# The score products of a channel tile's two heads, issued as six matmuls in turn on rows 0-63 and 64-127

## The chip, the cores and the metric

The kernel runs on one core of one Trainium2 chip. The metric is the device time of one launch in microseconds (us), median of the runs. Engines: PE is TensorE (its weight loads are listed apart as PEld), DVE VectorE, ACT ScalarE, POOL GpSimd, SP the engine that issues most DMAs. Each engine works through its own instructions in order; they wait for one another by semaphores.

## The reference: what is computed

One layer of a decoder for a prompt of 512 tokens and 8 sample tokens, width 2048. One input projection gives queries, keys and values (16 heads of 64 channels), indexer queries (16 heads of 64), one indexer key of 64 and a weight per indexer head, pooling inputs and gates. An indexer scores every visible key,

```
s = einsum('bthi,bsi->bths', qi, ki) * IDX_DIM ** -0.5
I = einsum('bths,bth->bts', relu(s), wi)
```

and each prompt token keeps the 128 best keys of its causal range. Attention over these (scores q.k / 8, softmax, times v), a pooling mixer, two gates, an output projection and a feed-forward network of width 8192 with squared ReLU follow. For the prompt the kernel computes all scores of a block of 128 queries against the keys up to that block's end (128, 256, 384 or 512 of them) and adds a bias of -1e30 where a key was not kept.

## The kernel before

All products are made of three matmuls: each operand is split into a high and a low part, and high x high, low x high and high x low are summed in one PSUM bank. Projections come in units of 128 output channels: 16 k-slots (`unit`, L1811), in each of which three products go into two halves of 260 tokens, six matmuls of 260 columns in all; for indexer queries (`index_unit`, L1835) three matmuls of 392 columns in one piece, since the first 128 tokens keep all their keys and need no scores. Channels lie on the 128 partitions, so a channel tile of a query or key holds two heads: head 0 on rows 0-63, head 1 on rows 64-127.

Other work of PE is put between the k-slots by hand, as hooks: PE's instructions have the order in which they are written.

**Indexer stage** (some 175 to 290 us). For channel tile j (8 of them) and query block i = 1, 2, 3 with 256, 384 and 512 keys, `index_steps` issues one step for each head: `split_product`, three matmuls of 64 rows (L1821), in the order `ISTEPS` (all i of head 0, then all i of head 1), at k-slots 4, 6, 8, 10, 12, 14 of the next tile's unit. Step c = 6j + n writes bank c % 4. ACT takes it with a Relu into buffer c % 4 (L798, `s_irl`), DVE multiplies by the head's weight and adds to the block's bias (L1387, `s_iac`). PE waits until the Relu of step c - 4 is done, ACT until the addition of step c - 4 is done, DVE until its own addition three steps before is done. ACT makes the high part of the next weights (L731) and POOL the low part (L1100) in the same stage.

**Attention rounds** (some 440 to 870 us). Four rounds, each with two channel tiles. Eight units run in a round (two each of q, k, v and a gate), and 16 score steps x = 0 to 15 (`STEPS`: tile jj, block i = 0 to 3, head hh innermost) hang between their k-slots. The list `TIMELINE` holds due times in k-slots: score step x is due at 77.3 + 2.8 x, its exponential 1.5 later, its transposes ("turn", L2004) 4.9 later, the product with the values ("pv", L2011) 8.2 or 9.1 later, and after both heads of a block the transpose of the output ("oT", L2017) 10.0 after the odd step. PE, ACT and DVE each issue their parts in the order of this list. Score step x writes bank x % 2; DVE adds the bias and takes the maximum (L1471, signalled by `s_mx`, which stands one ahead), ACT makes the exponential in place (L863), PE transposes it, DVE copies it (L1479). Before score step x PE waits for `s_mx` = max(x, 1), which means that the maximum of step x - 2 is done and its bank is free.

Of the kernel before, what the change touches and what calls it, by code (L numbers as in the profile page):

```python
# [32 lines left out]
P = 128  # L33
# [7 lines left out]
HD = 64  # L41
# [50 lines left out]
def program(nc, x_prompt, x_sample, cache_k, cache_v, cache_kidx, state_pool, page_table, norm_mix_g, w_in,  # L92
# [5 lines left out]
    def sem(name):  # L98
        return ctx.enter_context(nc.semaphore(name))
# [8 lines left out]
    def at(name, shape, dt, off):  # L108
        return nc.alloc_sbuf_tensor_at(name, shape, dt, offset=base + off)
# [42 lines left out]
    qih = at("qih", [P, NJ, SEQ], F32R, R2)  # L152
    qil = at("qil", [P, NJ, SEQ], F32R, R2 + 16640)
# [22 lines left out]
    kih = at("kih", [P, SEQ], F32R, SM + 1312)  # L176
    kil = at("kil", [P, SEQ], F32R, SM + 1312 + 2048)
    qh = at("qh", [P, 2, SEQ], F32R, R2C + 5120)
    ql = at("ql", [P, 2, SEQ], F32R, R2 + 16640)
    kh = at("kh", [P, 2, SEQ], F32R, R2 + 20736)  # L180
    kl = at("kl", [P, 2, SEQ], F32R, R2 + 24832)
# [91 lines left out]
    AB = ctx.enter_context(nc.psum_tensor("AB", [P, 4, 512], F32))  # L273
# [67 lines left out]
    s_isc = sem("indexer_products")  # L341
    s_irl = sem("indexer_relu")
    s_iac = sem("indexer_accumulated")
# [10 lines left out]
    s_sc = sem("scores_ready")  # L354
    s_mx = sem("scores_maximum_ready")
# [144 lines left out]
    def qi_sample(rows, slot):  # L500

        few = HC - HP
        return PP[rows, slot, 0, HP - P:QI_N].rearrange("p (a b) -> p a b", b=few)[:, 0:HC // few + 1:HC // few, :]

    ISTEPS = [(i, hh) for hh in range(2) for i in range(1, 4)]

    STEPS = [(jj, i, hh) for jj in range(2) for i in range(4) for hh in range(2)]

# [210 lines left out]
    def _(act):  # L719
# [71 lines left out]
        def index_relus(j):  # L791
            for n, (i, hh) in enumerate(ISTEPS):
                c = 6 * j + n
                act.wait_ge(s_isc, c + 1)
                if c >= 4:
                    act.wait_ge(s_iac, c - 3)
                w = P * (i + 1)
                act.activation(rl[c % 4][:, 0:w], AB[:, c % 4, 0:w], ACT.Relu).then_inc(s_irl, 1)  # L798
# [461 lines left out]
    def _(dve):  # L1260
# [82 lines left out]
        for j in range(NJ):  # L1343
            u, g = 2 * N_U + j, j // 2
            w = 2 << g
# [22 lines left out]
        for j in range(NJ):  # L1368
            u = 2 * N_QI + j
            dve.wait_ge(s_ps[j // 2], 16)  # L1370
            dve.wait_ge(s_qih, j + 1)
            for to, cols in QI_PROMPT:
                dve.tensor_tensor(qil[:, j, to], PP[:, u % 2, 0, cols], qih[:, j, to].bitcast(F32), ALU.subtract)
            dve.tensor_copy(qiB[0:HD, 0, 0, j, :].rearrange("p (f c) -> p f c", f=2), qi_sample(slice(0, HD), u % 2))
            dve.tensor_copy(qiB[HD:P, 1, 1, j, :].rearrange("p (f c) -> p f c", f=2), qi_sample(slice(HD, P), u % 2))\
                .then_inc(drained[u % 2], 1)
            if j == 0:
                group_out(3)
            for n, (i, hh) in enumerate(ISTEPS):
                c, w = 6 * j + n, P * (i + 1)  # L1380
                col = wN[:, i, hh * 8 + j:hh * 8 + j + 1]
                dve.wait_ge(s_irl, c + 1)
                if j + hh == 0:
                    ins = dve.tensor_scalar(blk_bias[i], rl[c % 4][:, 0:w], col, None, ALU.mult)
                else:
                    dve.wait_ge(s_iac, c - 2)
                    ins = dve.scalar_tensor_tensor(out=blk_bias[i], in0=rl[c % 4][:, 0:w], scalar=col,  # L1387
                                                   in1=blk_bias[i], op0=ALU.mult, op1=ALU.add)
                ins.then_inc(s_iac, 1)
# [45 lines left out]
        with dve.Fori(0, QKV_IT) as it:  # L1435
            order.enter(it, 16)
            for t, kind, x in TIMELINE:
                if kind == "drain" and x[0] < 6:
                    u, jj = 2 * N_QKV + x[0], x[0] % 2
# [26 lines left out]
                elif kind == "score":  # L1466
                    jj, i, hh = STEPS[x]
                    w = P * (i + 1)
# [5 lines left out]
                elif kind == "turn":  # L1474
                    jj, i, hh = STEPS[x]
                    w = P * (i + 1)
# [3 lines left out]
                elif kind == "pv":  # L1480
                    jj, i, hh = STEPS[x]
# [4 lines left out]
                elif kind == "oT":  # L1486
                    jj, i, hh = STEPS[x]
# [31 lines left out]
        for g in range(2 * NB):  # L1519
            b, f = g // 2, g % 2  # L1520
# [268 lines left out]
    def _(pe):  # L1789
# [25 lines left out]
                    if hooks and e == 0 and k in hooks:  # L1815
                        hooks[k]()

        def split_product(out, sta, stas, mov, movs):

            for n, (a, b) in enumerate(((0, 0), (1, 0), (0, 1))):  # L1820
                mm = pe.matmul(out, sta(stas[a]), mov(movs[b]), start=(n == 0), stop=(n == 2))  # L1821
            return mm

        def z(k):
            return zh[:, k], zl[:, k]
# [16 lines left out]
        def before(u):  # L1842
            return [(u + 1) // 2, u // 2]
# [59 lines left out]
            unit(2 * N_U + j, "wide", z, before(2 * N_U + j), hooks=hooks)  # L1903

        def index_steps(j):
            def step(n):
                i, hh = ISTEPS[n]
                c, r = 6 * j + n, HD * hh
                if n == 0:
                    pe.wait_ge(drained[j % 2], (2 * N_QI + j) // 2 + 1)  # L1910
                if c == 0:
                    pe.wait_ge(s_grpd, 4)
                    pe.wait_ge(s_kid, 32)
                if c >= 4:
                    pe.wait_ge(s_irl, c - 3)
                split_product(AB[:, c % 4, 0:P * (i + 1)], lambda t: t[r:r + HD, j, P * i:P * i + P], (qih, qil),
                              lambda t: t[r:r + HD, 0:P * (i + 1)], (kih, kil)).then_inc(s_isc, 1)

            return {4 + 2 * n: (lambda n=n: step(n)) for n in range(6)}

        for j in range(NJ):
            hooks = index_steps(j - 1) if j else {}
# [45 lines left out]
        for m in range(2, 6):  # L1968
            b = 2 * m - 4
# [6 lines left out]
        for it in range(0, QKV_IT):  # L1976
            def a3_turn(kind, x):
                pe.wait_ge(s_a3d, it * A3_PER + (A3_AT[(kind, x)] + 1))

            def side(kind, x):  # L1980
                if kind == "knat":
                    a3_turn(kind, x)
                    pe.wait_ge(drained[x % 2], it * 4 + ((2 * N_QKV + 2 + x) // 2 + 1))
                    for t in range(4):
                        mm = pe.transpose(AB[:, 3, P * t:P * t + P], kT[:, x, P * t:P * t + P], ident[:, :])
                    mm.then_inc(s_a3, 1)
                elif kind == "vnat":
                    a3_turn(kind, x)
                    pe.wait_ge(drained[x % 2], it * 4 + ((2 * N_QKV + 4 + x) // 2 + 1))
                    for t in range(4):  # L1990
                        mm = pe.transpose(AB[:, 3, P * t:P * t + P], vT[:, P * t:P * t + P], ident[:, :])
                    mm.then_inc(s_a3, 1)
                elif kind == "score":
                    jj, i, hh = STEPS[x]
                    pe.wait_ge(s_mx, it * 16 + max(x, 1))
                    r = HD * hh
                    split_product(AB[:, x % 2, 0:P * (i + 1)], lambda t: t[r:r + HD, jj, P * i:P * i + P], (qh, ql),
                                  lambda t: t[r:r + HD, jj, 0:P * (i + 1)], (kh, kl)).then_inc(s_sc, 1)
                elif kind == "turn":
                    jj, i, hh = STEPS[x]  # L2000
                    pe.wait_ge(s_ex, it * 16 + (x + 1))
                    pe.wait_ge(s_ptd, it * 16 + (x + 1))
                    for t in range(i + 1):
                        mm = pe.transpose(AB[:, 2, P * t:P * t + P], pr[:, x % 2, P * t:P * t + P], ident[:, :])  # L2004
                    mm.then_inc(s_pt, 1)
                elif kind == "pv":
                    jj, i, hh = STEPS[x]
                    a3_turn(kind, x)
                    pe.wait_ge(s_ptd, it * 16 + (x + 2))
                    for t in range(i + 1):  # L2010
                        mm = pe.matmul(AB[:, 3, 0:HD], pT[:, x % 2, P * t:P * t + P],  # L2011
                                       vn[:, jj, t, HD * hh:HD * hh + HD], start=(t == 0), stop=(t == i))
                    mm.then_inc(s_a3, 1)
                elif kind == "oT":
                    jj, i, hh = STEPS[x]
                    a3_turn(kind, x)
                    pe.transpose(AB[:, 3, 0:P], on[:, i, :], ident[:, :]).then_inc(s_a3, 1)  # L2017

            events = [(k, x) for _, k, x in TIMELINE if k not in ("drain", "top", "exp")]

            groups, unit_of = {}, None
            for k, x in events:
                if k == "unit":
                    unit_of = x
                    groups[x] = []
                else:
                    groups[unit_of].append((k, x))
            for n in range(8):
                hooks = {s: (lambda g=groups[(n, s)]: [side(k, x) for k, x in g]) for s in range(16) if groups[(n, s)]}
                unit(2 * N_QKV + n, "wide", z, before(2 * N_QKV + n), it, 8, 4, hooks)  # L2030
# [191 lines left out]
        for t in range(5):  # L2222
# [4 lines left out]
            for m in range(0 if t else KD - 2, KD):  # L2227
                mm = y_turn(t, m)
# [30 lines left out]
```

## Time and profile before

| | |
|---|---|
| median of 3 runs (lowest, highest) | 2936.05 us (2935.62, 2936.62) |
| the profiled execution | 2935.32 us |
| its span, first to last instruction | 2933.6 us |
| PE busy | 2856.2 us (97%) |
| DVE busy | 1425.0 us (49%) |
| ACT, POOL busy | 863.7, 858.1 us (29% each) |
| mean granted clock of PE | 0.994 |

The busy time of PE is the time in which at least one matmul is in flight, not the time in which it does all it can. The row of a matmul gives its start as the profile records it, and an end that is modelled; the starts of neighbours tell more than the durations. "x2" in a row of the timeline stands for two like instructions behind one another, and the start is that of the first. `64*128 64x256` is a matmul with a stationary operand of 64 rows and 128 columns, and a moving operand of 64 rows and 256 columns. In brackets stands idle time of the engine ahead of an instruction, and what ended it.

### The profile page before, as it was taken

The page shows a single profiled execution, that of the slowest core. Times are in us where ns is not written, and L with a number is a line of the kernel's source. Part 1 is how long each engine was busy: PE and PEld are TensorE (multiplying, and loading weights), DVE is VectorE, ACT ScalarE, POOL GpSimd, SP SyncE. Part 2 cuts the span into 40 slices and gives each one's busy share as a digit, 9 for nine tenths or more (in the row PEclk, how much of TensorE's full clock was granted, in tenths as well). Part 3 has the DMA queues.
Part 4 walks back from the last instruction along what each step waited for, and adds up shares of the span by engine and source line. Part 5 has one row for each costly group of instructions (what it writes and reads, how often), then busy time and mean ns, then how long its engine had stood idle before and what let it go on. Part 6 is the DMA issues. An engine that isn't in the chain of part 4 may idle for free.

```text
span 2933.6 us, 53028 instructions
## 1 busy us (share of the span) xinstructions
PE 2856.2 (97%) x22735; PEld 2774.2 (95%) x22735; DVE 1425.0 (49%) x2194; ACT 863.7 (29%) x1063; POOL 858.1 (29%) x280
## 2 busy tenths in 40 slices
PE   6999999999999999999989999999999999999997
PEld 6988999999999989999979999999989999999997
DVE  4555863646545404332167777777763223222212
ACT  4133222222222114223343444444432222222212
POOL 2333432332326533433300000000024444444431
PEclk9999999999999999999999999999999999999999
DMA  5222332323227644434424344344363233332321
GB/s 187 98 83 91 99 98 76 98 69 101 69 76 258 201 144 141 130 127 130 127 80 137 117 144 133 120 145 127 126 225 137 87 116 116 116 134 97 116 101 59
DMA packets 268734, 354.75 MB, mean 121 GB/s; under 512 B 9706, under 2 KB 199346, under 8 KB 267225
## 3 DMA queue, kind: packets, MB, share of 16 engines
q1 hardware_dynamic: 232067, 296.01, 30.5%
q10 hardware_dynamic: 29262, 30.28, 3.1%
q0 software_dynamic: 7200, 25.30, 2.5%
q8 instruction: 180, 2.95, 0.4%
q14 instruction: 25, 0.20, 0.0%
HBM read 310.55 MB, written 41.19 MB: 120 GB/s over the span
## 4 chain that ended last, share of the span: by engine, by line
PE 84%; issue 6%; DVE 4%; POOL 2%; ACT 1%; DMA 1%; DVEq 1%; ACTq 0%; POOLq 0%; SPq 0%
PE PP L1811 53%; PE PP L2178 18%; PE AB L2178 3%; PE PP L1835 3%; PE AB L1821 3%; POOL lo L1100 2%; PE AB L2011 1%; PE AB L2069 1%; DVE prod L1523 1%; PE AB L2004 1%; DMA qb<-q_scratch 1%; PE AB L1896 0%; DVE craw L1730 0%; ACT AB L752 0%; DVE scS L1458 0%
## 5 line engine op out<-in xcount | busy, mean ns | idle before, releaser
L1100 POOL TENSOR_TENSOR lo<-raw,hi 128x2048 fp32r<-128x2048 f32 x168 | 798.8, 4755 | 1938.3 <-ACT hi L731 1257.7
L731 ACT ACTIVATE hi<-raw 128x2048 fp32r<-128x2048 f32 x168 | 321.3, 1913 | 627.0 <-PE PP L1811 608.5
L1811 PE MATMUL PP<-zh,hi 128*128 128x260 f32 x2080 | 442.5, 294 | 2.0 <-DVE dheld L1312 1.1
L1811 PE MATMUL PP<-fh,hi 128*128 128x260 f32 x2048 | 413.6, 283 | 7.2 <-issue 5.0
L1811 PE MATMUL PP<-zh,lo 128*128 128x260 f32 x2080 | 419.4, 283 | 0.0
L1811 PE MATMUL PP<-zl,hi 128*128 128x260 f32 x2080 | 419.2, 283 | 0.0
L1811 PE MATMUL PP<-fh,lo 128*128 128x260 f32 x2048 | 413.4, 284 | 0.0
L1811 PE MATMUL PP<-fl,hi 128*128 128x260 f32 x2048 | 412.7, 283 | 0.0
L1622 DVE TENSOR_TENSOR lo<-raw,hi 128x1024 fp32r<-128x1024 f32 x224 | 274.4, 1226 | 158.8 <-ACT hi L991 158.8
L1811 PEld LDWEIGHTS PP<-zh,hi 128*128 128x128 f32 x2080 | 320.6, 189 | 19.4 <-issue 14.7
L1763 DVE TENSOR_TENSOR h<-PP,h 128x520 f32<-128x520 f32 x128 | 89.5, 700 | 500.6 <-PE PP L1811 500.6
L1811 PEld LDWEIGHTS PP<-fh,hi 128*128 128x128 f32 x2048 | 316.2, 189 | 8.1 <-issue 6.4
L1811 PEld LDWEIGHTS PP<-zh,lo 128*128 128x128 f32 x2080 | 321.4, 189 | 0.0
L1811 PEld LDWEIGHTS PP<-zl,hi 128*128 128x128 f32 x2080 | 321.1, 189 | 0.0
L991 ACT ACTIVATE hi<-raw 128x1024 fp32r<-128x1024 f32 x224 | 237.2, 1061 | 279.0 <-DVE raw L1639 75.7
L1811 PEld LDWEIGHTS PP<-fh,lo 128*128 128x128 f32 x2048 | 316.5, 189 | 0.0
L1811 PEld LDWEIGHTS PP<-fl,hi 128*128 128x128 f32 x2048 | 315.5, 189 | 0.0
L742 ACT COPY held<-eps 1x1 f32<-1x1 f32 x113 | 21.3, 189 | 363.9 <-PE PP L1811 253.5
L1811 PE MATMUL PP<-mgh,hi 128*128 128x260 f32 x512 | 104.7, 286 | 0.1
L1811 PE MATMUL PP<-mgh,lo 128*128 128x260 f32 x512 | 103.1, 283 | 0.0
L1811 PE MATMUL PP<-mgl,hi 128*128 128x260 f32 x512 | 103.1, 283 | 0.0
L2178 PE MATMUL PP<-a,hi 128*128 128x260 f32 x512 | 95.3, 286 | 5.8 <-DVE stg L1692 5.8
(387 smaller groups left out, 5406.0 us busy)
## 6 DMA issues: line engine op xcount, KB each, us to landing
raw<-in_w_in_dram SPq DMA_DIRECT2D x36, 2048.0 KB, 9.0
raw<-in_w_up_dram SPq DMA_DIRECT2D x32, 2048.0 KB, 9.0
raw<-in_w_down_dram SPq DMA_DIRECT2D x32, 2048.0 KB, 8.0
ffn_scratch<-stg SPq DMA_DIRECT2D x32, 520.0 KB, 2.8
craw<-ffn_scratch SPq DMA_DIRECT2D x16, 1040.0 KB, 6.5
raw<-in_w_out_dram SPq DMA_DIRECT2D x8, 2048.0 KB, 9.7
gates_scratch<-gst ACTq DMA_DIRECT2D x32, 260.0 KB, 3.5
raw<-in_w_attn_out_dram SPq DMA_DIRECT2D x8, 1024.0 KB, 5.4
```

What stands on the lines that cost most here:

```text
L731: act.activation(part(hi, kind, u), raw_unit(kind, u), ACT.Copy).then_inc(hi_done, 1)
L991: act.activation(ring_hi[i % 4], up_weights(s, pos), ACT.Copy).then_inc(up_hi, 1)
L1100: pool.tensor_tensor(part(lo, kind, u), raw_unit(kind, u), part(hi, kind, u).bitcast(F32), ALU.subtract)\
L1523: dve.tensor_tensor(prod[:, :], kv[:, g % 4, :], qb[:, b % 2, :], ALU.mult).then_inc(s_kvu, 1)
L1622: dve.tensor_tensor(ring_lo[i % 4], up_weights(s, pos), ring_hi[i % 4].bitcast(F32), ALU.subtract)\
L1763: dve.tensor_tensor(hm, PP[:, e, :, 0:HC], hm, ALU.add).then_inc(drained[e], 1)
L1811: mm = pe.matmul(PP[:, slot, f, 0:HC], w[:, k, P * e:P * e + P], a[:, f, :], start=(k == 0 and n == 0), stop=(k == nk - 1 and n == 2))
L1821: mm = pe.matmul(out, sta(stas[a]), mov(movs[b]), start=(n == 0), stop=(n == 2))
L1835: mm = pe.matmul(PP[:, u % 2, 0, 0:QI_N], w[:, k, :], a, start=(k == 0 and n == 0), stop=(k == KD - 1 and n == 2))
L2004: mm = pe.transpose(AB[:, 2, P * t:P * t + P], pr[:, x % 2, P * t:P * t + P], ident[:, :])
L2011: mm = pe.matmul(AB[:, 3, 0:HD], pT[:, x % 2, P * t:P * t + P], vn[:, jj, t, HD * hh:HD * hh + HD], start=(t == 0), stop=(t == i))
L2178: mm = pe.matmul(out, w[:, k, :], a, start=(k == 0 and n == 0 and not onto), stop=(k == KH - 1 and n == 2), skip_group_check=onto or opens)
```

## The change

`split_product` goes, and `head_pair` comes in its place. It issues the three products of both heads in turn: high x high of head 0 on rows 0-63, the same of head 1 on rows 64-127, then low x high of both, then high x low of both. The two heads write two banks, and the last matmul of each head signals by itself.

In the indexer stage `ISTEPS` has the head innermost, so that the steps c and c + 1 are the two heads of one block. There are three pairs for a tile, at k-slots 4, 8 and 12. A pair waits until the Relus up to step c - 3 are done. DVE waits, for head 1, until its addition for head 0 (the instruction before) is done, and for head 0 until the one of the same block in the tile before.

In the attention rounds a pair is issued at the due time of its even step; at the odd one PE issues nothing. The pair waits until the maximum of step x - 1 is done, so that both banks are free. The orders of DVE and ACT stay.

```diff
--- before.py
+++ after.py
@@ -502,7 +502,7 @@
         few = HC - HP
         return PP[rows, slot, 0, HP - P:QI_N].rearrange("p (a b) -> p a b", b=few)[:, 0:HC // few + 1:HC // few, :]
 
-    ISTEPS = [(i, hh) for hh in range(2) for i in range(1, 4)]
+    ISTEPS = [(i, hh) for i in range(1, 4) for hh in range(2)]
 
     STEPS = [(jj, i, hh) for jj in range(2) for i in range(4) for hh in range(2)]
 
@@ -1383,7 +1383,7 @@
                 if j + hh == 0:
                     ins = dve.tensor_scalar(blk_bias[i], rl[c % 4][:, 0:w], col, None, ALU.mult)
                 else:
-                    dve.wait_ge(s_iac, c - 2)
+                    dve.wait_ge(s_iac, c if hh else c - 4)
                     ins = dve.scalar_tensor_tensor(out=blk_bias[i], in0=rl[c % 4][:, 0:w], scalar=col,
                                                    in1=blk_bias[i], op0=ALU.mult, op1=ALU.add)
                 ins.then_inc(s_iac, 1)
@@ -1815,11 +1815,14 @@
                     if hooks and e == 0 and k in hooks:
                         hooks[k]()
 
-        def split_product(out, sta, stas, mov, movs):
+        def head_pair(outs, sta, stas, mov, movs, done):
 
             for n, (a, b) in enumerate(((0, 0), (1, 0), (0, 1))):
-                mm = pe.matmul(out, sta(stas[a]), mov(movs[b]), start=(n == 0), stop=(n == 2))
-            return mm
+                for hh, out in enumerate(outs):
+                    rows = slice(HD * hh, HD * hh + HD)
+                    mm = pe.matmul(out, sta(stas[a], rows), mov(movs[b], rows), start=(n == 0), stop=(n == 2))
+                    if n == 2:
+                        mm.then_inc(done, 1)
 
         def z(k):
             return zh[:, k], zl[:, k]
@@ -1903,20 +1906,20 @@
             unit(2 * N_U + j, "wide", z, before(2 * N_U + j), hooks=hooks)
 
         def index_steps(j):
-            def step(n):
-                i, hh = ISTEPS[n]
-                c, r = 6 * j + n, HD * hh
-                if n == 0:
+            def step(m):
+                i, c = m + 1, 6 * j + 2 * m
+                w = P * (i + 1)
+                if m == 0:
                     pe.wait_ge(drained[j % 2], (2 * N_QI + j) // 2 + 1)
                 if c == 0:
                     pe.wait_ge(s_grpd, 4)
                     pe.wait_ge(s_kid, 32)
                 if c >= 4:
-                    pe.wait_ge(s_irl, c - 3)
-                split_product(AB[:, c % 4, 0:P * (i + 1)], lambda t: t[r:r + HD, j, P * i:P * i + P], (qih, qil),
-                              lambda t: t[r:r + HD, 0:P * (i + 1)], (kih, kil)).then_inc(s_isc, 1)
-
-            return {4 + 2 * n: (lambda n=n: step(n)) for n in range(6)}
+                    pe.wait_ge(s_irl, c - 2)
+                head_pair([AB[:, (c + hh) % 4, 0:w] for hh in range(2)], lambda t, r: t[r, j, P * i:P * i + P],
+                          (qih, qil), lambda t, r: t[r, 0:w], (kih, kil), s_isc)
+
+            return {4 + 4 * m: (lambda m=m: step(m)) for m in range(3)}
 
         for j in range(NJ):
             hooks = index_steps(j - 1) if j else {}
@@ -1992,10 +1995,11 @@
                     mm.then_inc(s_a3, 1)
                 elif kind == "score":
                     jj, i, hh = STEPS[x]
-                    pe.wait_ge(s_mx, it * 16 + max(x, 1))
-                    r = HD * hh
-                    split_product(AB[:, x % 2, 0:P * (i + 1)], lambda t: t[r:r + HD, jj, P * i:P * i + P], (qh, ql),
-                                  lambda t: t[r:r + HD, jj, 0:P * (i + 1)], (kh, kl)).then_inc(s_sc, 1)
+                    if hh == 0:
+                        w = P * (i + 1)
+                        pe.wait_ge(s_mx, it * 16 + (x + 1))
+                        head_pair([AB[:, x, 0:w] for x in range(2)], lambda t, r: t[r, jj, P * i:P * i + P],
+                                  (qh, ql), lambda t, r: t[r, jj, 0:w], (kh, kl), s_sc)
                 elif kind == "turn":
                     jj, i, hh = STEPS[x]
                     pe.wait_ge(s_ex, it * 16 + (x + 1))
```

## Rows read from the trace of the kernel before

**Rows 1.** Busy time by stretch: length, PE, PEld, DVE, ACT, POOL, clock, DMA.

```profile
175.00:290.00 115.00, 114.91 (x581) 90.73 (x582) 55.79 (x76) 41.70 (x72) 33.77 (x12) 1.00 0.25 80
440.00:870.00 430.00, 426.54 (x3332) 403.32 (x3330) 229.71 (x621) 106.66 (x184) 123.99 (x27) 1.00 0.26 83
```

**Rows 2.** The page's chain of waits, shares of the span by line.

```profile
PE PP L1811 53%; PE PP L2178 18%; PE AB L2178 3%; PE PP L1835 3%; PE AB L1821 3%; POOL lo L1100 2%; PE AB L2011 1%; PE AB L2069 1%; DVE prod L1523 1%; PE AB L2004 1%; DMA qb<-q_scratch 1%; PE AB L1896 0%; DVE craw L1730 0%; ACT AB L752 0%; DVE scS L1458 0%
```

**Rows 3.** Timeline of PE, first score step; columns: start, duration, engine, line, operation.

```profile
442.07 0.41 PE L1811 MATMUL PP<-zh,lo 128*128 128x260 f32 x2
442.40 0.32 PE L1821 MATMUL AB<-kh,qh 64*128 64x128 f32 x1
442.57 0.27 PE L1821 MATMUL AB<-kh,ql 64*128 64x128 f32 x1
442.68 0.27 PE L1821 MATMUL AB<-kl,qh 64*128 64x128 f32 x1
442.88 0.51 PE L1811 MATMUL PP<-zh,hi 128*128 128x260 f32 x2
443.23 0.40 PE L1811 MATMUL PP<-zl,hi 128*128 128x260 f32 x2
```

**Rows 4.** Timeline of PE, indexer steps of 256 and 512 keys.

```profile
188.85 0.34 PE L1835 MATMUL PP<-zh,lo 128*128 128x392 f32 x1
189.12 0.38 PE L1821 MATMUL AB<-kih,qih 64*128 64x256 f32 x1
189.35 0.28 PE L1821 MATMUL AB<-kih,qil 64*128 64x256 f32 x1
189.47 0.27 PE L1821 MATMUL AB<-kil,qih 64*128 64x256 f32 x1
...
189.96 0.34 PE L1835 MATMUL PP<-zl,hi 128*128 128x392 f32 x1
...
192.66 0.34 PE L1835 MATMUL PP<-zh,lo 128*128 128x392 f32 x1
192.93 0.49 PE L1821 MATMUL AB<-kih,qih 64*128 64x512 f32 x1
193.26 0.39 PE L1821 MATMUL AB<-kih,qil 64*128 64x512 f32 x1
193.49 0.39 PE L1821 MATMUL AB<-kil,qih 64*128 64x512 f32 x1
...
194.10 0.34 PE L1835 MATMUL PP<-zl,hi 128*128 128x392 f32 x1
```

**Rows 5.** Timeline of PE's weight loads, first score step.

```profile
442.51 0.19 PEld L1821 LDWEIGHTS AB<-kh,ql 64*128 64x128 f32 x1
442.62 0.19 PEld L1821 LDWEIGHTS AB<-kl,qh 64*128 64x128 f32 x1
```

**Rows 6.** Timeline of all engines: step 11's maximum ends, score step 12 starts.

```profile
482.68 0.08 DVE L1471 DVE_READ_ACCUMULATOR2_ANT nm<- 128x1 f32 x1
...
484.46 0.44 PE L1821 MATMUL AB<-kh,qh 64*128 64x384 f32 x1
```

**Rows 7.** Timeline of all engines: end of step 0's exponential, its transpose.

```profile
444.86 0.19 ACT L863 ACTIVATION_READ_ACCUMULATOR pr<-pr,nm 128x1 f32 x1
...
447.69 0.27 PE L2004 MATMUL AB<-ident,pr 128*128 128x128 f32 x1
```

**Rows 8.** Timeline of all engines: POOL's subtraction and DVE's additions in the indexer stage.

```profile
189.00 4.57 POOL L1100 TENSOR_TENSOR lo<-raw,hi 128x2048 fp32r<-128x2048 f32 x1 [13.06 <-ACT hi L731]
...
190.19 4.19 DVE L1387 SCALAR_TENSOR_TENSOR bias<-rl,wN,bias 128x256 f32<-128x256 f32 x2 [2.12 <-ACT rl L798]
```

**Rows 9.** Timeline of PE: transposes on rows 0-63 and 64-79 in turn.

```profile
59.41 0.27 PE L1880 MATMUL AB<-ident,kiT 64*128 64x64 f32 x1
59.62 0.23 PE L1881 MATMUL AB<-ident,wiT 16*128 16x16 f32 x1
59.78 0.27 PE L1880 MATMUL AB<-ident,kiT 64*128 64x64 f32 x1
```

## The prediction

> **What bounds the kernel now.** I first read the table of stretches, because a change to two stages is worth what those stages are bound by. In the indexer stage (175 to 290 us) TensorE (PE) is busy 114.91 of 115.00 us, in the four attention rounds (440 to 870 us) 426.54 of 430.00, while the next engine, VectorE (DVE), has 55.79 and 229.71 [rows 1]. Matmul ends are modelled, so I don't take that as full speed; it says only that PE is hardly ever without work in flight. The chain of waits comes second: it runs along PE, and the score products (L1821) are 3% of the span by themselves, some 88 us [rows 2]. So what PE saves there comes off the total, unless a wait takes its place. Third come the single instructions, where the price of a score step can be read. The granted clock is 1.00 in both stretches, the 2.4 GHz level [rows 1], so these times need no correction.
>
> **One step before.** A step is three matmuls of 64 rows between matmuls of 128 rows. Its price is the time from the last wide matmul ahead of it to the second one behind it, less those wide ones at their own pitch. The pitch by width comes from second to third matmul of a step: 0.11 us at 128 columns, 0.12 at 256, 0.23 at 512 [rows 3, 4], so some 0.12 for the 260-column and 0.18 for the 392-column neighbours.
> - 128 columns: 442.07 to 443.23 is 1.16, less four wide ones (two rows of x2), 0.48: 0.68 us [rows 3].
> - 256: 188.85 to 189.96 is 1.11, less two, 0.36: 0.75 [rows 4].
> - 512: 192.66 to 194.10 is 1.44, less 0.36: 1.08 [rows 4]. 384 I put halfway, 0.92.
>
> The indexer has 8 tiles x 2 heads of each of 256, 384 and 512; attention has 4 rounds x 2 tiles x 2 heads of each of the four widths: 16 steps of 128 and 32 of each other. Sum 16 x 0.68 + 32 x 2.75 = 98.9 us, in 112 steps.
>
> Three matmuls at their own pitch are only 0.33, 0.36, 0.53 (pitch halfway, 0.175) and 0.69 us. The other 0.35 to 0.39 us of each step is paid for going to 64 rows and back: the first matmul stands 0.33 us (442.07 to 442.40) behind two wide ones that take 0.24, its weight load starts only with it, so that the second comes 0.17 later where the third follows in 0.11, and the same happens on the way out (0.20, then 0.35 for two) [rows 3]. That is about 42 us in 112 steps.
>
> **What the change removes.** Two steps of equal width become one of six matmuls. Half of the goings and returns vanish: 56 x 0.35 to 0.39 us. This needs no overlap at all.
>
> **What it may overlap.** Neighbours now lie on different rows and in different banks. No row before shows two such matmuls of equal height behind one another, so the cost of alternating is bounded from both sides:
> - Least: the partner is free. Then six cost what three do.
> - Most: each switch between the halves is paid like a change of height. The nearest rows are transposes that alternate between 64 rows from 0 and 16 rows from 64: starts 0.21 and 0.16 us apart though 64 and 16 columns flow [rows 9]. Less the flow (0.00043 us a column, from 0.12 and 0.23 above) that is about 0.165 us a switch.
> - I take a value between: matmuls of the two halves run beside each other, but weight loads follow one another at 0.11 us, as they do inside a step (442.51, 442.62) [rows 5]. I choose this because the step's own rows have the same height, operand type and stationary width, while the transposes change the height at each switch.
>
> Under it the sixth matmul starts after six loads, 0.66 us behind the first load; at 512 columns after 0.22 and two flows of 0.23, 0.68. The third started at 0.28 (load bound, so three loads more, 0.33), 0.35, 0.455 and 0.56 [rows 3, 4]. So six cost 0.33, 0.31, 0.21 and 0.12 us more than three: 1.01, 1.06, 1.13 and 1.20. Against two steps (1.36, 1.50, 1.84, 2.16) a pair saves 0.35, 0.44, 0.71 and 0.96 us. With 8 pairs of 128 and 16 of each other width: 8 x 0.35 + 16 x 2.11 = 36.6 us.
>
> A rule bears on the choice, and what follows in this paragraph is not used in the sum. The Trainium skill ("TensorEngine Tiling (Array Packing)", Key Properties) says that changing the tiling mode, "not just tile", drains the engine. By that rule the transposes above are dear because 16 and 64 rows are different modes, and two halves of 64 rows are the same mode: no switch price, and the sum stays 36.6 us or better. By the row alone it would be the loss of the fourth rival.
>
> **What it adds: waits.** In attention the pair at an even step a now waits for the maximum of step a-1, where step a waited for that of a-2. Behind it on PE stand all projection matmuls, and POOL, ACT and DVE wait for those. The tightest case before: DVE finished the maximum's last part at 482.68 + 0.08, and PE began the next score at 484.46: 1.70 us to spare [rows 6]. The maximum of a-1 can only come earlier, since its product moves ahead by one step. PE gets there earlier by at most the removed step, 1.08 us. I cost it at nothing.
>
> The odd product leaves the stretch between an even step's product and its transposes; these wait for ACT's exponential. At step 0 that ended at 444.86 + 0.19, and the transpose began at 447.69 [rows 7]: 2.64 us, more than the 0.68 to 1.08 that go. Nothing new is late there. DVE and ACT keep their order; for an odd step they only get data earlier.
>
> In the indexer PE waits for the two Relus of two pairs ago, with eight k-slots (24 matmuls of 0.18, 4.3 us) between. DVE now adds two heads of one block behind each other; the added wait is on its own previous instruction, and behind it stand the next additions and ACT's Relus, which reuse the same four buffers. POOL's subtraction (189.00, 4.57 us) keeps the first addition open: two additions take 4.19 us from 190.19, to 194.38 [rows 8]. In the new order the first pair's additions would end near 194.4 too; the third pair's Relus, which need these buffers, come two pairs (two of 1.1 and two of 2.1, 6.4 us) after 189.12 [rows 4], at 195.5 or later. Cost: zero; without that cover, up to the 1 us between, eight times, 8 us. The two completion signals of a pair were there before, one in each step; no DMA issue is moved past another.
>
> **Sum.** The profiled execution took 2935.32 us, its span 2933.6 and 1.7 around it; the median of the runs is 2936.05, 0.73 above. 2935.3 - 36.6 = 2898.7; as a median 2899.4 us.
>
> **Rivals.**
> 1. No overlap: the halves queue behind one another and only the goings and returns are saved. Six matmuls cost three pitches more (0.33, 0.36, 0.53, 0.69), a pair saves 0.35 at 128 and 0.39 else: 2.8 + 18.7 = 21.5 us, 2914.6. For it: all rows before show matmuls one by one. Against: none of them had different rows to use.
> 2. Loads overlap too: the partner's load runs beside its neighbour's, so six cost what three did. A pair saves 0.68, 0.75, 0.92, 1.08: 5.4 + 44.0 = 49.4 us, 2886.7. For it: a load of rows 0-63 doesn't touch rows 64-127. Against: every pair of loads in the trace is at least 0.11 apart, whatever its height [rows 5].
>  The Trainium skill has this as a rule (the same page and section): different tiles can execute weight loads and matmuls in parallel. No run before shows it.
> 3. A new wait binds: the pair waits for a maximum that comes late. 28 pairs (7 in each round) at 1 us would give back 28 of 36.6 us, 2927.4. Against: 1.70 us to spare at the tightest [rows 6].
> 4. Slower: each switch between the halves drains the array, at the 0.165 us of the transposes plus the flow: 0.22, 0.275, 0.33 and 0.385 a matmul. Five such gaps in place of the two of a step (0.28, 0.35, 0.455, 0.56) make a pair 1.50, 1.775, 2.115 and 2.445 us, 0.14, 0.275, 0.275 and 0.285 more than two steps: 1.1 + 13.4 = 14.5 us, 2950.6. It takes place inside the pair, and loses as soon as a switch costs over about 0.08 us more than the hidden one (a saved return of 0.39 against five switches). For it: [rows 9]. Against: there the height changes too.
>
> **How the numbers follow.** Forecast 0.42, loads overlap 0.27, no overlap 0.14, drain 0.08, a new wait 0.05, and 0.04 that gains and losses cancel. The forecast, the second and the first rival hold 0.83, so the range runs from 2884 to 2918, a few us beyond their ends; the forecast's own is 2893 to 2906. This kernel's measurement can tell about 0.2%, 5.9 us: all cases but the drain and the cancelling one are faster by more, which gives 0.87 faster (part of the waits left out), 0.04 the same and 0.09 slower.
>
> **What would show it.** In the changed profile a pair should be six matmuls of 64 rows between wide ones, with one entry of some 0.33 and one exit. Inside, loads 0.11 apart and matmuls of the two halves starting 0.11 apart at all widths would be the forecast; 512-column starts 0.23 apart the first rival; loads of two halves nearly together the second; each load starting only with its own matmul, 0.2 to 0.4 apart, the fourth. PE idle ahead of a score, released by DVE, would be the third. The two stretches should be shorter by some 17 us each (attention 19.7, indexer 16.9), and nothing elsewhere; a gain in the stretches given back behind 870 us would make the prediction wrong though each step holds.

## The result, and the profile after

The changed kernel takes 2887.99 us, median of 4 runs (2887.08 to 2892.11), against 2935.84 us for the kernel before (2933.33 to 2936.62, 4 runs): a ratio of 0.9836, 95% interval 0.9824 to 0.9847, or 47.9 us less. The profiled execution took 2887.97 us, its span is 2886.2.

The same two stages in the table of stretches of the kernel after (columns as in [rows 1]), each taken from its first score or transpose to its last (the rounds, in both kernels, to 0.7 us ahead of it):

```profile
174.60:267.60 93.00, 92.96 (x581) 80.93 (x582) 55.90 (x76) 39.04 (x72) 33.73 (x12) 1.00 0.31 99
398.70:827.60 428.90, 424.41 (x3532) 411.89 (x3533) 245.91 (x647) 109.79 (x189) 133.19 (x29) 1.00 0.27 84
```

By the same marks the kernel before has 175.1 to 290.0 (114.9 us) and 421.1 to 876.0 (454.9 us). So the indexer stage gave 21.9 us and the attention rounds 26.0, together 47.9. The two profiled spans differ by 47.4 (2933.6 and 2886.2): the first stage begins 0.5 us sooner, the time between the stages is the same 131.1, and behind the rounds the kernel after is 1.0 us longer. So next to nothing was given back elsewhere. In the page's chain of waits by line the score products fall from 3% [rows 2] to 1%:

```profile
PE PP L1811 55%; PE PP L2182 18%; PE AB L2182 3%; PE PP L1838 3%; POOL lo L1100 2%; PE AB L1823 1%; PE AB L2015 1%; PE AB L2073 1%; DMA qb<-q_scratch 1%; PE AB L2008 1%; PE AB L1899 0%; DVE prod L1523 0%; ACT AB L752 0%; DVE craw L1730 0%; DVE scS L1458 0%
```

Timeline of PE, kernel after, the first attention pair (128 columns) and an indexer pair of 512. A row of x2 is now one matmul of each head:

```profile
419.67 0.41 PE L1811 MATMUL PP<-zh,lo 128*128 128x260 f32 x2
420.00 0.33 PE L1823 MATMUL AB<-kh,qh 64*128 64x128 f32 x2
420.17 0.28 PE L1823 MATMUL AB<-kh,ql 64*128 64x128 f32 x2
420.28 0.27 PE L1823 MATMUL AB<-kl,qh 64*128 64x128 f32 x2
420.49 0.51 PE L1811 MATMUL PP<-zh,hi 128*128 128x260 f32 x2
420.83 0.41 PE L1811 MATMUL PP<-zl,hi 128*128 128x260 f32 x2
...
191.64 0.34 PE L1838 MATMUL PP<-zh,lo 128*128 128x392 f32 x1
191.91 0.50 PE L1823 MATMUL AB<-kih,qih 64*128 64x512 f32 x2
192.25 0.40 PE L1823 MATMUL AB<-kih,qil 64*128 64x512 f32 x2
192.48 0.40 PE L1823 MATMUL AB<-kil,qih 64*128 64x512 f32 x2
...
193.09 0.34 PE L1838 MATMUL PP<-zl,hi 128*128 128x392 f32 x1
```

Set beside [rows 3, 4]: the three starts are as far apart as those of a single step (0.17 and 0.11; 0.34 and 0.23), only each stands for two. A pair of 128 costs 419.67 to 420.83, 1.16, less 0.48 for four wide ones: 0.68 us, the price of one step before. A pair of 512 costs 1.45 less 0.36: 1.09, against 1.08. By the same reckoning 256 has 0.74 (197.01 to 198.11) and 384 has 0.92 (188.58 to 189.86). The second head is free. The weight loads of a later 128-column pair say the same; six start at three times, 0.11 us apart:

```profile
445.01 0.19 PEld L1823 LDWEIGHTS AB<-kh,qh 64*128 64x128 f32 x2
445.12 0.19 PEld L1823 LDWEIGHTS AB<-kh,ql 64*128 64x128 f32 x2
445.23 0.19 PEld L1823 LDWEIGHTS AB<-kl,qh 64*128 64x128 f32 x2
```

Theory A, tested below: the partner on the other 64 rows costs nothing, its load and its flow lie beside its neighbour's, and the price of going to 64 rows and back is paid once for two heads.

### The profile page after: what moved, and what is told of

The parts are those of the page before. It is cut to its first block, busy times and chain, and to the rows that moved or that the text cites. A ratio compares the mean times of both kernels' runs of the same rounds, so it can differ in the third digit from the quotient of the medians.

```text
span 2886.2 us, 53028 instructions
## 1 busy us (share of the span) xinstructions
PE 2807.7 (97%) x22735; PEld 2748.3 (95%) x22735; DVE 1424.3 (49%) x2194; ACT 861.1 (30%) x1063; POOL 859.5 (30%) x280
## 4 chain that ended last, share of the span: by engine, by line
PE 84%; issue 6%; DVE 4%; POOL 2%; ACT 1%; DMA 1%; DVEq 1%; ACTq 0%; POOLq 0%; SPq 0%
PE PP L1811 55%; PE PP L2182 18%; PE AB L2182 3%; PE PP L1838 3%; POOL lo L1100 2%; PE AB L1823 1%; PE AB L2015 1%; PE AB L2073 1%; DMA qb<-q_scratch 1%; PE AB L2008 1%; PE AB L1899 0%; DVE prod L1523 0%; ACT AB L752 0%; DVE craw L1730 0%; DVE scS L1458 0%
```

## The experiments

Four kernels on one chip (the kernel before took 2938.08 us there, and the ratios are to that) test what the gain hangs on.

**Same rows.** In `head_pair`:

```diff
-                    rows = slice(HD * hh, HD * hh + HD)
+                    rows = slice(0, HD)
```

> Both members of a pair read rows 0-63, still six matmuls in turn in one burst and into two banks; head 1's scores are left out (head 0's stand in their place). Theory A (the partner on other rows costs nothing, its load and its flow lie beside its neighbour's): nothing can lie beside, six cost three pitches more than three, 0.33, 0.36, 0.53 and 0.69 us at 128, 256, 384 and 512 columns; 8 x 0.33 + 16 x 1.58 = 27.9 us over the changed kernel, 2916 us. Theory B (two banks in turn, or the merging of two steps alone, bring the gain): as the changed kernel, 2888 us.

Measured 2918.17 us, ratio 0.9936 (0.992 to 0.9953): some 30 us over the changed kernel. The timeline of PE at a pair of 512:

```profile
194.15 0.33 PE L1838 MATMUL PP<-zh,lo 128*128 128x392 f32 x1
194.42 0.72 PE L1823 MATMUL AB<-kih,qih 64*128 64x512 f32 x2
194.98 0.63 PE L1823 MATMUL AB<-kih,qil 64*128 64x512 f32 x2
195.45 0.63 PE L1823 MATMUL AB<-kil,qih 64*128 64x512 f32 x2
...
196.30 0.34 PE L1838 MATMUL PP<-zl,hi 128*128 128x392 f32 x1
```

Two products now take 0.56 and 0.47 us where they took 0.34 and 0.23, and the pair costs 2.15 less 0.36: 1.79 us. Two banks and one burst for two heads bring 20 us, the first rival's 21.5; the other 28 hang on the different rows. Theory A holds, theory B falls.

**Head after head.**

```diff
-            for n, (a, b) in enumerate(((0, 0), (1, 0), (0, 1))):
-                for hh, out in enumerate(outs):
+            for hh, out in enumerate(outs):
+                for n, (a, b) in enumerate(((0, 0), (1, 0), (0, 1))):
```

> The same six matmuls on the same rows and banks in one burst, but the three of head 0 first and then the three of head 1. Theory A: only the first of head 1 can lie beside the last of head 0, because matmuls start in order; five starts apart in place of three, two pitches more, 0.22, 0.24, 0.35 and 0.46 us a pair: 8 x 0.22 + 16 x 1.05 = 18.6 us over the changed kernel, 2907 us. If the queue could let the second head run ahead: 2888. If nothing lies beside unless the rows alternate at every instruction: 27.9 us more, 2916.

Measured 2890.69 us, ratio 0.9841 (0.9824 to 0.9857), the same as with heads in turn. The number that I took for theory A, 2907, was wrong, as I had put into it that matmuls start in order. The timeline of PE, sorted by start:

```profile
191.55 0.34 PE L1838 MATMUL PP<-zh,lo 128*128 128x392 f32 x1
191.82 0.51 PE L1823 MATMUL AB<-kih,qih 64*128 64x512 f32 x2
192.16 0.40 PE L1823 MATMUL AB<-kih,qil 64*128 64x512 f32 x2
192.40 0.40 PE L1823 MATMUL AB<-kil,qih 64*128 64x512 f32 x2
...
193.01 0.34 PE L1838 MATMUL PP<-zl,hi 128*128 128x392 f32 x1
```

The program has high x high, low x high, high x low of head 0 and then the same of head 1; they started two by two. The second start of each x2 lies 0.01 us behind the first. Head 1's first matmul went past two older ones to free rows. The pair costs 1.46 less 0.36: 1.10 us. So what counts here is that the other half's work stands close behind, not that it alternates.

**Uneven rows.**

```diff
-                    rows = slice(HD * hh, HD * hh + HD)
+                    rows = slice(HD * hh, HD * hh + HD // (1 + hh))
```

> Head 1's matmuls read 32 rows (64-95) where head 0's read 64, so the height changes at every instruction of a pair; half of head 1's channels are left out. If a change of height is what made the alternating transposes of the kernel before dear: five gaps of 0.22, 0.275, 0.33 and 0.385 us, a pair costs 1.50, 1.78, 2.12 and 2.45 in place of 0.68, 0.75, 0.92 and 1.09, 8 x 0.82 + 16 x 3.59 = 64 us over the changed kernel, 2952 us. If those were dear because they wrote one bank or are transposes: 2888 us.

Measured 2985.63 us (2976.94 to 2990.06), ratio 1.0169 (1.0151 to 1.0187): slower than before. The timeline of PE at a pair of 256, and the stretch that holds the attention rounds:

```profile
190.91 0.33 PE L1838 MATMUL PP<-zh,lo 128*128 128x392 f32 x1
191.17 0.70 PE L1823 MATMUL AB<-kih,qih 64*128 64x256 f32 x2
191.80 0.70 PE L1823 MATMUL AB<-kih,qil 64*128 64x256 f32 x2
192.42 0.70 PE L1823 MATMUL AB<-kil,qih 64*128 64x256 f32 x2
...
193.33 0.34 PE L1838 MATMUL PP<-zl,hi 128*128 128x392 f32 x1
```

```profile
440.00:920.00 480.00, 475.12 (x3526) 439.20 (x3526) 245.44 (x651) 112.78 (x189) 130.23 (x29) 0.98 0.24 75
```

Every matmul now takes 0.31 us of the pair (191.17 to 193.05 for six), and the pair costs 2.06 us in place of 0.74, more than the 1.78 that the transposes [rows 9] gave. The second matmul of the pair, of 32 rows, shows singly:

```profile
191.48 0.38 PE L1823 MATMUL AB<-kih,qih 32*128 32x256 f32 x1
```

It starts 0.31 us behind the one of 64 rows (191.17), and the next of 64 rows 0.31 behind it (191.80). So the price is paid in both directions, and isn't that of low matmuls as such. Half the rows, so less work, but two heights in turn: the fourth rival's price is real, and its condition is the change of height.

The time exceeds the expected 2952 us by 34, and most of that is the size of the price. By the same reckoning pairs of 128, 384 and 512 cost 1.72, 2.41 and 2.75 us: some 0.20 us a switch beside the flow, where [rows 9] gave 0.165. That makes 80 us over the changed kernel and not 64. The profiled execution, the fastest of the four (2976.94), is 89 us over it. The rounds' granted clock is 0.98 there, with stretches at the 1.2 GHz level (514.2 to 517.6 us: 0.51), and 1.00 in the changed kernel; 480 us at 0.98 are some 9 us more, about what is left. The slower three runs have a mean clock of 0.986 or 0.987 in place of 0.990.

**Full rows.**

```diff
-                    rows = slice(HD * hh, HD * hh + HD)
+                    rows = slice(0, P)
```

> Both members of a pair read all 128 rows, so no matmul changes the height; the scores are sums over both heads' channels, the separate ones are left out. If the 0.35 to 0.39 us beside the flow of each burst are paid for the change from 128 to 64 rows and back: six matmuls cost only their pitches, 0.66, 0.72, 1.05 and 1.38 us in place of 0.68, 0.75, 0.92 and 1.09: 16 x 0.39 less 0.2 = 6 us over the changed kernel, 2894 us. If they are paid for the hook itself (its waits ahead of the first matmul): 56 x 0.37 = 21 us more, 2915 us.

Measured 2898.86 us, ratio 0.9868 (0.9851 to 0.9884), 11 us over the changed kernel (9 by the ratios) and 8 over the one with head after head on the same chip. 6 were expected, and its own four runs lie 6 us apart (2895.25 to 2901.42). The timeline of PE at a pair of 384:

```profile
189.97 0.34 PE L1838 MATMUL PP<-zh,lo 128*128 128x392 f32 x1
190.15 0.51 PE L1823 MATMUL AB<-kih,qih 128*128 128x384 f32 x2
190.50 0.51 PE L1823 MATMUL AB<-kih,qil 128*128 128x384 f32 x2
190.84 0.51 PE L1823 MATMUL AB<-kil,qih 128*128 128x384 f32 x2
...
191.36 0.34 PE L1838 MATMUL PP<-zl,hi 128*128 128x392 f32 x1
```

The first score stands 0.18 behind the last wide matmul, the ordinary pitch, where a 64-row pair has 0.27; the waits ahead of it are the same. Six cost 1.39 less 0.36: 1.03 us, their bare pitch. The 0.35 to 0.39 us of a burst are paid for the height, not for the hook.

Four more on one chip (the kernel before took 2937.46 us there), the changed kernel among them.

> The changed kernel once more, to compare the next three with on one chip: 2888 us, 0.9836 of the kernel before.

Measured 2889.33 us, ratio 0.9835 (0.9821 to 0.9848).

**Indexer only.** At the score event of the attention rounds, the single step of before:

```diff
-                    if hh == 0:
-                        w = P * (i + 1)
-                        pe.wait_ge(s_mx, it * 16 + (x + 1))
-                        head_pair([AB[:, x, 0:w] for x in range(2)], ...)
+                    pe.wait_ge(s_mx, it * 16 + max(x, 1))
+                    split_product(AB[:, x % 2, 0:P * (i + 1)], ...).then_inc(s_sc, 1)
```

> Pairs in the indexer stage alone; the attention rounds issue single steps as before. Theory A (half of the steps' own price goes, stage by stage): attention gives back 8 x (0.68 + 0.75 + 0.92 + 1.09) = 27.5 us less the 1 us that its four new waits for the value drain cost, 2914.5 us. If the gain of one stage was paid back in the other (a queue or DVE work that moves from one to the other), the sum of the parts would differ: under 2910 or over 2920.

Measured 2914.66 us, ratio 0.9917 (0.9904 to 0.9931): the indexer alone saves 22.8 us and leaves 25.3 to the attention rounds. In its trace the indexer stage takes 93.0 us, as in the changed kernel (174.6 to 267.6), and the rounds 454.9, as in the kernel before (398.7 to 853.6). So neither part pays for the other. The four new waits of the changed kernel are gone here too; the cause that the expectation gives for them, the value drain, is corrected below.

**Two pairs in one burst.**

```diff
-            return {4 + 4 * m: (lambda m=m: step(m)) for m in range(3)}
+            return {4: two, 12: lambda: step(2)}
```

where `two` issues step 0 and step 1, and step 0 waits until all Relus of the tile before are done.

> In the indexer stage the pairs of 256 and 384 keys of a tile stand in one burst of twelve matmuls at k-slot 4, in all four banks; the pair of 512 stays at k-slot 12. Theory A: eight goings to 64 rows and back fewer, 8 x 0.38 = 3.0 us less, 2885 us. Rival: the four Relus and additions behind one another hold the banks, PE waits ahead of the pair of 512, nothing is gained or some us are lost, 2888 us or more.

Measured 2886.95 us, ratio 0.9826 (0.9812 to 0.9839): 2.4 us under the changed kernel in this comparison, with intervals that overlap. The timeline of PE shows the gain without that doubt:

```profile
185.85 0.34 PE L1838 MATMUL PP<-zh,lo 128*128 128x392 f32 x1
186.12 0.38 PE L1823 MATMUL AB<-kih,qih 64*128 64x256 f32 x2
186.35 0.28 PE L1823 MATMUL AB<-kih,qil 64*128 64x256 f32 x2
186.47 0.28 PE L1823 MATMUL AB<-kil,qih 64*128 64x256 f32 x2
186.58 0.33 PE L1823 MATMUL AB<-kih,qih 64*128 64x384 f32 x2
186.76 0.34 PE L1823 MATMUL AB<-kih,qil 64*128 64x384 f32 x2
186.93 0.34 PE L1823 MATMUL AB<-kil,qih 64*128 64x384 f32 x2
...
187.49 0.34 PE L1838 MATMUL PP<-zl,hi 128*128 128x392 f32 x1
```

Twelve matmuls cost 1.64 less 0.36: 1.28 us, where the two pairs cost 0.74 and 0.92 apart. That is 0.38 us in each of 8 tiles, 3.0 us. Its median is the lowest of all versions tried.

**Values one slot later**, on top of that:

```diff
-            ev.append((16 * (5 + jj) + 2.2, "vnat", jj))
+            ev.append((16 * (5 + jj) + 3.2, "vnat", jj))
```

> As the one before, and the transposes of the values are due one k-slot later. In the changed kernel PE waits some 0.25 us there in each of four rounds, because DVE has not emptied the unit's bank yet; with 0.7 us more it should not: 1.0 us less, 2884 us. Rival: the wait moves to what stands behind it, no difference.

Measured 2891.48 us, ratio 0.984 (0.9826 to 0.9853), 4.5 us slower than the one before. The waits of PE name what came in:

```profile
PE AB L2021 <- DVE vn L1464: 4.0, 4, 1.0
```

The value transposes now stand right ahead of a product with the values (L2021 here), which needs the same bank, so PE waits 1.0 us in each round until DVE has copied it; the slots between had hidden that. The wait moved to what stands behind it and grew. The cause that I gave for the old wait was wrong as well: the waits of the weight loads below put it down to DVE's output copy (L1484), not to the emptying of the unit's bank.

**Six after six.** The burst of two pairs with head 0's six matmuls first:

```diff
+                for hh in range(2):
+                    r = slice(HD * hh, HD * hh + HD)
+                    for m in range(2):
+                        ...
+                        for n, (q, k) in enumerate(((qih, kih), (qil, kih), (qih, kil))):
+                            mm = pe.matmul(AB[:, (c + 2 * m + hh) % 4, 0:w], q[r, j, P * i:P * i + P], k[r, 0:w], ...)
+                mm.then_inc(s_isc, 4)
```

> As the kernel with two pairs in one burst, but the burst has the six matmuls of head 0 first and then the six of head 1 (one signal for all four products on the last). With three after three the second head started 10 ns behind the first. If a matmul on free rows may start past six that stand ahead of it: 2885 us as with two pairs in turn. If it may not pass more than three: the second head starts 0.3 us later, 8 x 0.35 = 2.8 us more, 2888. If it can't pass six at all: head 1 runs behind head 0, 8 x 0.89 = 7.1 us more, 2892 us.

Measured 2889.75 us, ratio 0.9835 (0.9818 to 0.9851). The four runs (2887.20 to 2895.06) take in two of the three expected times, so the trace has to decide. The timeline of PE:

```profile
185.69 0.34 PE L1838 MATMUL PP<-zh,lo 128*128 128x392 f32 x1
185.96 0.38 PE L1937 MATMUL AB<-kih,qih 64*128 64x256 f32 x1
186.19 0.28 PE L1937 MATMUL AB<-kih,qil 64*128 64x256 f32 x1
186.30 0.28 PE L1937 MATMUL AB<-kil,qih 64*128 64x256 f32 x1
186.31 0.44 PE L1937 MATMUL AB<-kih,qih 64*128 64x256 f32 x2
...
186.65 0.28 PE L1937 MATMUL AB<-kil,qih 64*128 64x256 f32 x1
...
186.77 0.34 PE L1937 MATMUL AB<-kil,qih 64*128 64x384 f32 x1
...
187.66 0.34 PE L1838 MATMUL PP<-zl,hi 128*128 128x392 f32 x1
```

Head 0's first two matmuls run alone. Head 1's first starts 0.01 us behind head 0's third, past the three that still stand ahead of it. The burst costs 1.97 less 0.36, 1.61 us against 1.28: 0.33 more in 8 tiles, 2.6 us, as expected for "not more than three". Whether three is a limit of its own, or head 1's instructions came too late to go past more, these runs don't tell.

## Why the prediction was right in its range and wrong in its likeliest case

- **What bounds the kernel**: right. 47.9 us left the two stages and 47.4 left the span.
- **The price of a step, and what of it belongs to the height**: right. Full rows took the 0.35 to 0.39 us away, same rows kept one of two.
- **The term that failed**: "weight loads follow one another at 0.11 us". It made six matmuls cost 0.33, 0.31, 0.21 and 0.12 us more than three; measured is 0.00, -0.01, 0.00 and 0.01. The saving of a pair is 0.68, 0.76, 0.92 and 1.07 us in place of 0.35, 0.44, 0.71 and 0.96; with 8 and 16 pairs 49.4 us, not 36.6. That was the second rival, at 0.27 and 2886.7 us; the range held the result because it had been drawn to hold that rival too. The error was in the reading: every row with 0.11 between loads [rows 5] is of loads into the same rows, or of 128, and says nothing of a load into others. Nor is every pair of loads "at least 0.11 apart, whatever its height": two loads of 8 rows in the kernel before start at 889.93 and 889.98 (L2036, L2037). The rule that I set beside the second rival (the Trainium skill, "TensorEngine Tiling (Array Packing)", Key Properties: different tiles can execute weight loads and matmuls in parallel) agrees with this trace: six loads at three starts, 0.22 us from the first to the last.
- **Height against half**: right. The rule that a change of mode drains and a change of tile doesn't (the Trainium skill, the same page and section) agrees with both measurements, 0.31 us a matmul at 256 columns with two heights, and 0.12 for two with one.
- **The added waits**: nearly right. No score waits for a maximum of DVE, with 1.70 us to spare before [rows 6], and the indexer stage keeps PE busy for 92.96 of 93.00 us. But I followed the odd product's leaving only to the transposes of the probabilities, and not to those of the values. The waits of PE's weight loads in the attention rounds (columns: engine, line, releaser, line: us in total, times, longest), kernel after:

```profile
PEld AB L2021 <- DVE on L1484: 2.4, 4, 0.6
PEld AB L1994 <- DVE on L1484: 1.2, 4, 0.3
```

and kernel before:

```profile
PEld AB L2017 <- DVE on L1484: 2.4, 4, 0.6
```

 The first row answers to the last, the output's transposes at the end of a round. The second, the value transposes (L1994), is new: 1.2 us. Without the odd step between, PE comes there before DVE's output copy is done. The rounds gave 26.0 us where 8 x (0.68 + 0.75 + 0.92 + 1.08) = 27.4 were to be had by the second rival's prices; this wait, 1.2 us, is about the difference. With the odd steps back in the rounds (indexer only) the value transposes wait for no output copy. In the indexer stage 22.0 us were to be had by the same prices, and 21.9 came.

## What to carry to other kernels

Where a matmul uses 64 rows and another of the same height on the other 64 rows can stand close behind it, write them into one burst and into two banks: here the second cost nothing, load included, and the change of height was paid once for both. (Two heads in one bank were not tried.) Keep the heights equal, and put as many such matmuls as the banks allow between two changes. Before costing an overlap by a pitch from the trace, ask whether the rows behind that pitch shared the resource that the change separates.

## What the runs showed of the hardware that I had not expected

PE starts matmuls on other rows ahead of older ones, so what is said above of engines, that each works through its own instructions in order, doesn't hold for these starts. Three after three ran two by two (a pair of 512 at 1.10 us against 1.09 in turn); in six after six head 1 started only when three of head 0 were still ahead of it. With one signal for each product the order of the signals would then not be that of the program by itself: in six after six the last matmul of head 1's product of 256 columns started at 186.65, and that of head 0's product of 384, which stands ahead of it in the program, at 186.77.

Half the rows for one head made the kernel 1.7% slower than before rather than faster: changing the height between neighbours cost more (0.31 us a matmul at 256 columns) than the halved rows could save, and the granted clock of the attention rounds was 0.98 in place of 1.00.
